# Recurrence of a two-direction mixer: the two directions of a pair in step, or half a pair apart

## What is computed

```python
def step(state, inp):
    r_t, w_t, k_t, v_t, kk_t, a_t = inp
    sk = jnp.einsum('bhij,bhj->bhi', state, kk_t)
    state = (state * w_t[:, :, None, :]
             - sk[..., :, None] * (kk_t * a_t)[:, :, None, :]
             + v_t[..., :, None] * k_t[:, :, None, :])
    y = jnp.einsum('bhij,bhj->bhi', state, r_t)
    return state, y
...
for d in range(2):
    ...
    y = y + wkv7_scan(rh, hs(decay), kd, vh, kk, ah, reverse=(d == 1))
```

## Time and profile before

| | us |
|---|---|
| median of 3 runs | 2754.36 (2751.97 to 2762.08) |
| the profiled execution, time | 2756.88 |
| the profiled execution, span | 2755.1 |
| TensorE busy in the span | 2542.9 (92%) |
| VectorE busy | 1570.6 (57%) |
| ScalarE busy | 1164.2 (42%) |
| GpSimd busy | 910.2 (33%) |
| the recurrence, from its first instruction to the next stage's | 645.9 to 1034.5 |

### The profile page before, as it was taken

One profiled execution on the slowest core, in us unless ns is written; L12 is line 12 of the kernel. 1 busy time (PEld: TensorE's weight loads), 2 busy tenths in 40 slices (PEclk: granted clock), 3 DMA queues, 4 the chain that ended last, 5 costly groups with the idle time before them and its releaser, 6 DMA issues. The chain is left out here.

```text
span 2755.1 us, 51491 instructions
## 1 busy us (share of the span) xinstructions
PE 2542.9 (92%) x21459; PEld 2051.3 (74%) x21459; DVE 1570.6 (57%) x2264; ACT 1164.2 (42%) x1818; POOL 910.2 (33%) x623
## 2 busy tenths in 40 slices
PE   5998989796999999979999999996988999999998
PEld 4776656475888886768888888775776888888887
DVE  7775632367565646655555564455565555556445
ACT  5211243454555543444434444463443444444434
POOL 2301122103221202237787730001324777772000
PEclk7999999898999999989999999998998999999999
DMA  7687434712323224122222255551222322226554
GB/s 239 220 278 226 157 140 166 227 26 66 83 62 86 59 72 146 69 77 77 84 92 75 87 221 186 170 164 69 87 77 69 92 79 83 92 77 236 188 178 146
DMA packets 295914, 346.27 MB, mean 126 GB/s; under 512 B 28383, under 2 KB 224212, under 8 KB 295684
## 3 DMA queue, kind: packets, MB, share of 16 engines
q1 hardware_dynamic: 286044, 336.64, 37.3%
q10 hardware_dynamic: 9640, 6.33, 0.7%
HBM read 271.58 MB, written 71.34 MB: 124 GB/s over the span
## 5 line engine op out<-in xcount | busy, mean ns | idle before, releaser
L3074 POOL TENSOR_TENSOR cg_u_lo<-cg_u_raw,cg_u_hi 128x512 fp32r<-128x512 f32 x210 | 314.8, 1507 | 147.7 <-ACT cg_u_hi L2960 147.7
L131 PE MATMUL cg_ps<-m_hi,cg_u_hi 128*128 128x512 f32 x844 | 331.6, 393 | 25.3 <-DVE cg_u_lo L3149 21.0
L133 PE MATMUL cg_ps<-m_hi,cg_u_lo 128*128 128x512 f32 x844 | 330.3, 391 | 0.0
L132 PE MATMUL cg_ps<-m_lo,cg_u_hi 128*128 128x512 f32 x808 | 316.0, 391 | 0.0
L2960 ACT ACTIVATE cg_u_hi<-cg_u_raw 128x512 fp32r<-128x512 f32 x216 | 132.5, 631 | 380.8 <-PE cg_ps L133 230.4
L131 PEld LDWEIGHTS cg_ps<-m_hi,cg_u_hi 128*128 128x128 f32 x844 | 159.8, 189 | 60.4 <-DVE cg_u_lo L3149 21.8
L131 PE MATMUL cg_ps<-over_y_tx,cg_u_hi 128*128 128x512 f32 x480 | 186.7, 389 | 0.0
L132 PE MATMUL cg_ps<-over_y_tx,cg_u_hi 128*128 128x512 f32 x480 | 186.7, 389 | 0.0
L133 PE MATMUL cg_ps<-over_y_tx,cg_u_lo 128*128 128x512 f32 x480 | 186.7, 389 | 0.0
L133 PEld LDWEIGHTS cg_ps<-m_hi,cg_u_lo 128*128 128x128 f32 x844 | 159.9, 189 | 33.6
L3126 DVE SCALAR_TENSOR_TENSOR cg_z<-cg_ps,top_conv_f,cg_z 128x1023 f32<-128x1023 f32 x88 | 112.9, 1283 | 116.3 <-ACT cg_z L2984 116.3
(11 more groups left out here) (477 smaller groups left out, 6209.5 us busy)
## 6 DMA issues: line engine op xcount, KB each, us to landing
cg_u_raw<-in_ffn_up SPq DMA_DIRECT2D x88, 512.0 KB, 5.1
cg_u_raw<-in_ffn_down SPq DMA_DIRECT2D x64, 512.0 KB, 4.7
qkv_mw<-in_ada_w SPq DMA_DIRECT2D x12, 2048.0 KB
over_f_d_raw<-in_ffn_down SPq DMA_DIRECT2D x48, 512.0 KB, 5.0
scr_act<-cg_z SPq DMA_DIRECT2D x44, 512.0 KB, 2.7
qkv_mw<-in_ada_w SPq DMA_DIRECT2D x8, 1024.0 KB, 11.6
next_w<-in_mix_in SPq DMA_DIRECT2D x16, 512.0 KB, 5.9
za_out<-in_ada_w SPq DMA_DIRECT2D x8, 1024.0 KB
```

The source lines that it names most:

```text
L131: nc.tensor.matmul(out, a_hi, b_hi, start=first, stop=False)
L132: nc.tensor.matmul(out, a_hi, b_lo, start=False, stop=False)
L133: return nc.tensor.matmul(out, a_lo, b_hi, start=False, stop=last)
L3074: G.tensor_tensor(u_lo[:, n % RING], source(g, i), u_hi[:, n % RING].bitcast(F32), ALU.subtract).then_inc(ulo_done, 1)
```

## The change

Directions run half a pair apart. Every engine's loop over pairs becomes a loop over half pairs h, from -1 to 16. In a half, direction a is at the levels of its pair p, and direction b goes from solve of its pair q through carry, opens and closes to turns, scores, lower and values of its pair q + 1; then they change places. The phases' own code is the same (VectorE's carry is called in two parts), and a call with a pair that doesn't exist does nothing. The factor work is spread over the half in the same way. Ahead of the loop only direction 0's factors of pair 0 are made; direction 1's follow in h = -1, and the filling of the level buffers stands behind the first factors of direction 0, on VectorE and on GpSimd. SP's loads follow the same order.

```diff
@@ -1506,18 +1506,18 @@
-            for m in range(1, NPAIR):
-                for g in range(2):
-                    if m >= 2:
-                        sp.wait_ge(rg_c[g], 2 * (m - 1))
-                    load_values(g, m)
-                for g in range(2):
-                    load_kx(g, m)
-                for g in range(2):
-                    load_rx(g, m)
-                for g in range(2):
-                    load_lw(g, m)
-                    load_aa(g, m)
+            load_kx(0, 1)
+            load_rx(0, 1)
+            for h in range(-1, 2 * NPAIR + 1):
+                a, p, b, q = h % 2, h // 2, 1 - h % 2, (h - 1) // 2
+                if 0 < p + 1 < NPAIR:
+                    if p >= 1:
+                        sp.wait_ge(rg_c[a], 2 * p)
+                    load_values(a, p + 1)
+                load_lw(b, q + 2)
+                load_aa(b, q + 2)
+                load_kx(a, p + 2)
+                load_rx(a, p + 2)
@@ -1717,42 +1717,35 @@
-            for m in range(NPAIR):
-                turn(0, m, 0)
-                turn(0, m, 1)
-                turn(1, m, 0)
-                scores(0, m, 0)
-                turn(1, m, 1)
-                scores(0, m, 1)
-                scores(1, m, 0)
-                scores(1, m, 1)
-                lower(0, m)
-                values(0, m)
-                lower(1, m)
-                turn_u(0, m, 0)
-                level_x(0, m, 0)
-                values(1, m)
-                turn_u(1, m, 0)
-                level_x(1, m, 0)
...
-                for i in range(1, NL):
-                    for g in range(2):
-                        turn_u(g, m, i)
-                        level_x(g, m, i)
-                    if i < NL - 1:
-                        for g in range(2):
-                            level_t(g, m, i)
-                for phase in (last_u, solve, carry):
-                    for g in range(2):
-                        phase(g, m)
-                for g in range(2):
-                    step_open(g, m, 1)
-                for g in range(2):
-                    step_open(g, m, 0)
-                    step_close(g, m, 0)
-                for g in range(2):
-                    step_close(g, m, 1)
+            for h in range(-1, 2 * NPAIR + 1):
+                a, p, b, q = h % 2, h // 2, 1 - h % 2, (h - 1) // 2
+                turn_u(a, p, 0)
+                level_x(a, p, 0)
+                solve(b, q)
+                level_t(a, p, 0)
+                carry(b, q)
+                turn_u(a, p, 1)
+                level_x(a, p, 1)
+                step_open(b, q, 1)
+                level_t(a, p, 1)
+                step_open(b, q, 0)
+                step_close(b, q, 0)
+                turn_u(a, p, 2)
+                level_x(a, p, 2)
+                step_close(b, q, 1)
+                level_t(a, p, 2)
+                turn(b, q + 1, 0)
+                turn(b, q + 1, 1)
+                turn_u(a, p, 3)
+                level_x(a, p, 3)
+                scores(b, q + 1, 0)
+                level_t(a, p, 3)
+                scores(b, q + 1, 1)
+                turn_u(a, p, 4)
+                level_x(a, p, 4)
+                lower(b, q + 1)
+                values(b, q + 1)
+                last_u(a, p)
@@ -1856,41 +1849,29 @@
...
-            for m in range(NPAIR):
-                for g in range(2):
-                    tokens(g, m, 0)
-                    tokens(g, m, 1)
-                for g in range(2):
-                    f_rates(g, m + 1)
-                for g in range(2):
-                    values(g, m)
-                    turn_u(g, m, 0)
...
-                for g in range(2):
-                    last_u(g, m)
-                for g in range(2):
-                    solved_z(g, m)
-                    solved_w(g, m)
-                for c in range(2):
-                    for g in range(2):
-                        out(g, m, c)
+            f_rates(0, 0)
+            f_exp_in(0, 0)
+            f_exp_before(0, 0)
+            f_exp_out(0, 0)
+            for h in range(-1, 2 * NPAIR + 1):
+                a, p, b, q = h % 2, h // 2, 1 - h % 2, (h - 1) // 2
+                turn_u(a, p, 0)
+                solved_z(b, q)
+                solved_w(b, q)
+                turn_u(a, p, 1)
+                f_rates(a, p + 1)
+                turn_u(a, p, 2)
+                out(b, q, 0)
+                out(b, q, 1)
+                tokens(b, q + 1, 0)
+                turn_u(a, p, 3)
+                tokens(b, q + 1, 1)
+                f_exp_in(a, p + 1)
+                f_exp_before(a, p + 1)
+                turn_u(a, p, 4)
+                f_exp_out(a, p + 1)
+                values(b, q + 1)
+                last_u(a, p)
@@ -1934,20 +1915,16 @@
-            for g in range(2):
-                f_products(g, 0)
+            f_products(0, 0)
+            f_rhos(0, 0)
+            f_kappas(0, 0)
             fill(X1)
-            for g in range(2):
-                f_rhos(g, 0)
-                f_kappas(g, 0)
             fill(XL[0] + XL[1])
-            for m in range(1, NPAIR):
-                for g in range(2):
-                    f_products(g, m)
-                pool.wait_ge(f_before[1], m + 1)
-                for g in range(2):
-                    f_rhos(g, m)
-                    f_kappas(g, m)
+            for h in range(-1, 2 * NPAIR + 1):
+                a, p = h % 2, h // 2
+                f_products(a, p + 1)
+                f_rhos(a, p + 1)
+                f_kappas(a, p + 1)
@@ -2004,15 +1981,17 @@
...
-            def carry(g, m):
+            def carry(g, m, part):
...
@@ -2095,43 +2074,36 @@
-            for g in range(2):
-                for step in (f_scan, f_centre, f_shift):
-                    step(g, 0)
-            for g in range(2):
-                for step in (f_edges, f_alphas, f_nbetas):
-                    step(g, 0)
-            fill()
+            for step in (f_scan, f_centre, f_shift):
+                step(0, 0)
             dve.wait_ge(tab_loaded, 48)
-            for m in range(NPAIR):
-                for g in range(2):
-                    f_scan(g, m + 1)
-                scores(0, m, 0)
-                scores(0, m, 1)
-                scores(1, m, 0)
...
-                for i in range(NL):
-                    for g in range(2):
-                        level_x(g, m, i)
-                    if i == 1:
-                        f_shift(0, m + 1)
-                    if i == 2:
-                        f_shift(1, m + 1)
-                    if i < NL - 1:
-                        for g in range(2):
-                            level_t(g, m, i)
-                    if i < 2:
-                        f_centre(i, m + 1)
-                for step in (f_edges, f_alphas, f_nbetas):
-                    for g in range(2):
-                        step(g, m + 1)
-                for g in range(2):
-                    carry(g, m)
-                for c in range(2):
-                    for g in range(2):
-                        advance(g, m, c)
+            for h in range(-1, 2 * NPAIR + 1):
+                a, p, b, q = h % 2, h // 2, 1 - h % 2, (h - 1) // 2
+                level_x(a, p, 0)
+                f_edges(b, q + 1)
+                f_alphas(b, q + 1)
+                level_t(a, p, 0)
+                carry(b, q, 0)
+                carry(b, q, 1)
+                level_x(a, p, 1)
+                f_nbetas(b, q + 1)
+                if h == -1:
+                    fill()
+                    f_scan(1, 0)
+                level_t(a, p, 1)
+                advance(b, q, 0)
+                level_x(a, p, 2)
+                advance(b, q, 1)
+                level_t(a, p, 2)
+                f_centre(a, p + 1)
+                f_scan(b, q + 2)
+                f_shift(a, p + 1)
+                level_x(a, p, 3)
+                scores(b, q + 1, 0)
+                level_t(a, p, 3)
+                scores(b, q + 1, 1)
+                level_x(a, p, 4)
+                lower(b, q + 1)
```

More of the change, by code:

```diff
@@ L1857, in f_exp_out @@
                 A(cc[g][:, :, :], cc[g][:, :, :], ACT.Exp, scale=-DECAY).then_inc(f_exp[g], 1)
-            for g in range(2):
-                f_rates(g, 0)
-            for g in range(2):
-                f_exp_in(g, 0)
-                f_exp_before(g, 0)
-                f_exp_out(g, 0)
-            for m in range(NPAIR):
-                for g in range(2):
-                    tokens(g, m, 0)
-                    tokens(g, m, 1)
-                for g in range(2):
-                    f_rates(g, m + 1)
-                for g in range(2):
-                    values(g, m)
-                    turn_u(g, m, 0)
-                for i in range(1, NL):
-                    for g in range(2):
-                        turn_u(g, m, i)
-                    if i == 1:
-                        f_exp_in(0, m + 1)
-                    if i == 2:
-                        f_exp_before(0, m + 1)
-                        f_exp_out(0, m + 1)
-                    if i == 3:
```

(60 more changed lines are left out.)

1 line of the change is left out of this document (removed).

## The result

The changed kernel takes 2762.59 us (median of 16 runs, 2756.22 to 2769.90), the kernel before 2753.77 in 16 runs beside it (2747.58 to 2762.33): a ratio of 1.003, interval 1.0019 to 1.0040. It is slower by 0.3%, where I had forecast 0.2% faster. The time lies in the range, 2733 to 2763, but only just, and the sign is the other one.

What follows compares the result with a forecast made beforehand. TensorE's order was taken to bound the recurrence stage. Pairs -12.1, ends +12.1 and first turn -5.3 took the profiled 2756.9 us to 2751.6; less 2.5 to the median, 2749 us, range 2733 to 2763.

Steps and rivals of the forecast that it cites:

- First turn: Start of the recurrence: the first turn waits less for VectorE's first factors, so it comes 5.3 us earlier.
- The half pair: Each of the fourteen full halves, h = 1 to 14, takes 21.6 us including 0.6 us of TensorE waits.
- carry for zt: In each half, TensorE's carry newly waits 0.47 us for ScalarE's copy of zt after solve.
- The price of a mode change: TensorE switching operand shapes: 0.15 us a change, five more changes a pair, adding 0.75 us a pair.
- Stalls kept: TensorE waits with "issue" as releaser and no cause shown: 7 us over the full pairs, expected to remain.
- rival B: The stalls go too, or the waits were overstated: 2738 us, at most 2732; chance 0.20.
- Waits for lw and in-order waits (rival D): Waits for lw should vanish; the rival: VectorE or ScalarE stands in line each half, 2769 us and up; chance 0.09.
- h = -1: Pipeline fill, from the first turn to the first turn_u: 12.6 us, bounds 11 and 15.
- h = 0: First half with levels, direction 0's chain alone: 18.5 us plus 1.5 for the lower clock, 20 us.
- Rival C: Pipeline ends cost more at TensorE's lower clock, h = 0 by 7 us: 2756, or 2760 with drains; chance 0.19 with E.
- h = 15 and 16: Pipeline drain, one direction's chain alone: 18.6 us and 10.4 us, together 29 us.
- rivals C and E: C: ends cost more at the lower clock; E: one direction's chain binds, so nothing changes in effect; joint chance 0.19.

Runs made afterwards that it cites:

- r2: The changed kernel, unaltered, profiled a second time; its recurrence stage took 387.6 us, against 391.3 in the first profiled execution.
- r1: The kernel before, unaltered, profiled a second time; its recurrence stage took 384.3 us, against 388.6 in the first profiled execution.
- e1: Changed kernel plus useless TensorE transpositions in the gaps where the pipeline fills and drains; 2750.39 us, ratio 0.9993 to the kernel before.
- e6: Kernel before, in its old order, plus 64 useless TensorE transpositions before the first turn; 2753.98 us, ratio 0.9999 to the kernel before.
- e9: Changed kernel with fillers at both ends, the next stage's early loads cut into 18 pieces over h = 14 and 15; 2752.10 us, ratio 0.9995.
- e4: Changed kernel with VectorE's score products and lower of direction 0, pair 0, moved ahead of direction 1's centring; 2757.55 us, ratio 1.0017 to the kernel before.
- e7: Changed kernel with end fillers, 40 more before the first turn, and VectorE's first score products ahead of direction 1's centring; 2753.91 us, ratio 0.9999.
- e10: Changed kernel with end fillers (12 in h = -1), scores first, and direction 1's VectorE and ScalarE factor work moved later; 2749.64 us, ratio 0.9989.

## Why the prediction was wrong

Step by step, for after and r2:

- **First turn**, -5.3: it comes 9.18 us into the stage in both, 14.59 before: -5.4. Right.
- **The half pair**, 21.6: undisturbed 21.29, five of the fourteen within 0.1. Right, with its one new wait: carry for zt, 0.24 us idle, 0.46 with the surcharge, forecast 0.47. The wait for T that I had put at 0.14 isn't there. The price of a mode change was too high by a misreading of the earlier trace rows: into and out of the opens the step is 0.56 both times, and the 0.52 stands between two blocks of 64x64. That is 0.09 a change and not 0.15, and (41.3 + 5 x 0.09)/2 is 20.9; measured is 21.29 less 0.46, 20.83. The Trainium skill ("TensorEngine Tiling (Array Packing)", Key Properties) says that a change of mode drains TensorE; whatever the drain is, here it costs no more than that.
- **Stalls kept**, 7: 10.5 in both by the halves' lengths, 7 to 14 in all kernels of the new order with whole loads. By the forecast's own measure, idle time and 0.22 for each, they are 9.8 and 8.2 in after and r2, for 7.0 and 7.8 in before and r1. The term was short by 1 to 3.5; rival B, that they go, did not come. Its reason was that the new order spreads the loads; but a fetch of 16 KB is due every 4.3 us (71 in 308.6), and loads that are spread can meet more of them. No run parts that from chance. In the sum for the body this error and the one before, 14 halves of 0.3 us less, cancelled: that 309.4 came true is luck.
- **Waits for lw and in-order waits (rival D)**: no wait for lw in the halves. Right.
- **h = -1**, 12.6 (11 to 15): 15.6. The queue on VectorE was named right, but the products start 11.2 us behind the first turn, where I had 8.8, since fill and scan take 4.10 and 2.28; the rest is TensorE's lower and values at the lower clock.
- **h = 0**, 20: 23.2 and 23.8. This is the first half of the step that failed. I walked the chain at full clock (18.5; e1 shows 18.8) and added 1.5 us for the clock. Rival C had the mechanism and "all 7" as its price; 4.4 to 5 were paid.
- **h = 15 and 16**, 29: 33.2 and 28.9. This is the other half: the clock wasn't in the term at all, nor in rival C. In after it fell and cost 4 us, as e1 (29.5) and the solve of nearly twice the length show; in r2 it did not fall.

In the profile of after: 3.0 + 3.2 + 4.2 for the ends, -0.8 for the halves with their stalls, and a stall of 1 us that I had kept in the first pair: 8.6 us late of the forecast, of which 7.4 are h = 0 and the drain and 2.4 VectorE's queue in h = -1. Most of it is one mistake: the terms of fill and drain were priced by the chain's length, while in h = 0 of both executions and in the drain of one TensorE itself ran at half rate. The trace had the row for it, for the first pair ran at 0.91; the clock belonged in the sum for both ends. A chance of 0.19 for rivals C and E was not a bad one, but as priced, at 7 us in h = 0 and none in the drain, C came true in part alone. The Trainium skill ("TensorE: Matmul & The Clock Gate", What's actually happening) says it as "the default state is throttled, and activity releases the throttle"; the rows of e1 and after agree: 1.00 in h = 0 with the transpositions, 0.73 without.

The other runs fit it. The granted clock over the whole kernel is 0.9609 in the mean of after's 16 runs, 0.9649 in 94 runs of before from the later sets: by (1 - clock) x 2 x the time that is 216 us at the lower level against 193. The stage accounts for 17 of the 23 us more (39.1 in the mean of after and r2, 22.3 of before and r1), and e1 has 0.9654, the clock of before.

**What stays open.** The medians of after and before are 8.8 us apart, the stages only 3.0 (389.5 and 386.5 in the mean of two profiled executions each). After's two profiled executions, 2756.8 and 2753.7 us, stand beside and below the fastest of its others (2756.2), those of before, 2756.9 and 2755.3, above its median; and e6 has a stage of 380.2 with the median of before. Nor is the rest constant: behind the stage the fourteen traces take 1720.6 to 1722.0 us, but e9 1723.7 and e4 1727.3. One stage thus foretells a median to some 5 us only. After itself was timed in one set of 16 runs; r2's single execution, in another set, is below all of them. The recurrence begins at 643.0 to 654.1 us in the fourteen traces, behind code that is the same in all; why, and whether it differs by kernel, no run here settles. So the lower clock at the ends is shown to cost 8 us in one trace and 5 in the other (against e1), and fillers at the ends to be worth 0.37% in the ratio (1.0030 to 0.9993); that the ends are all of the 8.8 us is not shown.

## What to carry to other kernels

A software pipeline pays at both ends, and can pay twice: once for the length of the lone chain, and again if the clock of TensorE falls in its gaps. Price each end at both levels of the clock, and where the trace shows the lower one, try useless matmuls in the gaps before giving up on the order: few enough not to delay the chain (e7's 48 did, e10's 12 did not), and up to the work itself (e6's stopped 4.45 us too early). When work is moved ahead on one in-order queue, look at what the other queues now wait for: of e4's gain of 5.4 us in h = -1, 2.5 went back in h = 0, where ScalarE stood in line.

## What the runs showed of the hardware

TensorE's instructions arrive in packets of 16 KB, one in 4.3 us here, and with loads in flight TensorE waits up to 2.4 us for one. A trace names that "issue"; the sign of it is that the stall ends 2.2 to 3.5 us behind the start of a fetch, 121 times out of 121. The burst of early loads costs some 3 us in this way, and cutting the factor loads alone gave the old order 0.42%, more than the change of order did in any version.
